# The rest of the modulation as reductions by output column on VectorE, and the low part of every third weight piece on GpSimd

## The reference, cut to what matters

```
mod   = silu(c)     @ w_mod[l] + b_mod[l]
mod_c = silu(c_ctx) @ w_mod[l] + b_mod[l]
shift, scale, gate = split(mod, 3)
x = rms_norm(h, pre_norm_g[l]) * (1 + scale) + shift
...
h = h + gate * rms_norm(y, post_norm_g[l])
```

## Time and profile before

| | |
|---|---|
| three runs | median 3389.24 us (3387.71 to 3394.56) |
| the profiled execution | 3387.43 us, span 3385.6 us, mean granted clock 0.929 |
| TensorE busy | 3040.6 us (90%) |
| VectorE busy | 1966.1 us (58%) |
| ScalarE busy | 1109.5 us (33%) |
| GpSimd busy | 784.2 us (23%) |

### The profile page before, as it was taken

The page is one execution under the profiler, slowest core; times in us unless marked ns, Lnnn a source line. Parts: engine busy times, 40 slices in busy tenths (PEclk is TensorE's granted clock), DMA queues, the critical chain, the costliest instruction groups (busy, mean ns, idle before and its releaser), DMA issues.

```text
span 3385.6 us, 40936 instructions
## 1 busy us (share of the span) xinstructions
PE 3040.6 (90%) x15813; PEld 2449.2 (72%) x15813; DVE 1966.1 (58%) x2774; ACT 1109.5 (33%) x1774; POOL 784.2 (23%) x641
## 2 busy tenths in 40 slices
PE   6789778989978997998998996987999999999998
PEld 1167567777766886767786785764588999999887
DVE  5477876666665544444525455877554666666444
ACT  2132322322312323332423243222343444444443
POOL 0068448577462000000000000655200000000000
PEclk9989889989988999999999997988589899999999
DMA  8844224244333453323333253432033455555655
GB/s 310 279 141 155 75 97 146 97 143 146 110 121 109 171 170 113 116 78 107 108 101 114 78 184 103 142 98 77 14 120 129 141 185 181 186 182 182 197 194 168
DMA packets 148802, 471.19 MB, mean 139 GB/s; under 512 B 16752, under 2 KB 17776, under 8 KB 147440
## 3 DMA queue, kind: packets, MB, share of 16 engines
q1 hardware_dynamic: 137664, 431.03, 38.9%
q10 hardware_dynamic: 8384, 28.63, 2.2%
q0 software_dynamic: 2560, 8.91, 0.8%
HBM read 455.40 MB, written 13.11 MB: 138 GB/s over the span
## 4 chain that ended last, share of the span: by engine, by line
PE 56%; issue 18%; DVE 11%; POOL 7%; DMA 4%; ACT 3%; ACTq 0%; DVEq 0%; POOLq 0%; SPq 0%
PE bank L906 15%; PE bank L907 15%; PE bank L908 15%; POOL first_block_work L2306 3%; DMA common<-w_mod 2%; POOL common L2304 2%; DVE split_weights L1227 2%; PE bank L923 2%; ACT split_weights L1884 1%; DVE first_block_work L1325 1%; PE bank L1020 1%; PE bank L943 1%; PE bank L1098 1%; PE bank L1001 1%; DMA first_block_work<-w_mod_rows 1%
## 5 line engine op out<-in xcount | busy, mean ns | idle before, releaser
L1227 DVE TENSOR_TENSOR split_weights<-common,split_weights 128x1024 fp32r<-128x1024 f32 x628 | 831.5, 1332 | 789.1 <-ACT split_weights L1884 778.5
L1884 ACT ACTIVATE split_weights<-common 128x1024 fp32r<-128x1024 f32 x628 | 656.6, 1053 | 1155.5 <-PE bank L908 1098.0
L906 PE MATMUL bank<-split_weights,features 128*128 128x512 f32 x1920 | 820.6, 427 | 16.3 <-DVE features L1370 10.1
L907 PE MATMUL bank<-split_weights,features 128*128 128x512 f32 x1920 | 770.0, 401 | 0.0
L908 PE MATMUL bank<-split_weights,features 128*128 128x512 f32 x1920 | 769.3, 401 | 0.0
L2276 POOL TENSOR_TENSOR common<-common 128x1 f32<-128x1 f32 (+4 forms) x54 | 39.5, 739 | 1888.6 <-DVE common L1830 752.2
L906 PEld LDWEIGHTS bank<-split_weights,features 128*128 128x128 f32 x1920 | 375.0, 195 | 124.8 <-issue 37.0
L908 PEld LDWEIGHTS bank<-split_weights,features 128*128 128x128 f32 x1920 | 373.3, 194 | 82.7
L907 PEld LDWEIGHTS bank<-split_weights,features 128*128 128x128 f32 x1920 | 374.9, 195 | 79.6 <-issue 11.8
L906 PE MATMUL bank<-ffn_input_split,split_weights 128*128 128x256 f32 (+1 forms) x1376 | 393.1, 286 | 2.8 <-DVE ffn_input_split L1650 1.6
L907 PE MATMUL bank<-ffn_input_split,split_weights 128*128 128x256 f32 (+1 forms) x1376 | 391.6, 285 | 0.0
(11 more groups left out here) (282 smaller groups left out, 3677.2 us busy)
## 6 DMA issues: line engine op xcount, KB each, us to landing
common<-w_in SPq DMA_DIRECT2D x252, 512.0 KB, 3.4
common<-w_up SPq DMA_DIRECT2D x172, 512.0 KB, 4.2
first_block_work<-w_mod_rows SPq DMA_DIRECT2D x256, 256.0 KB, 3.6
common<-w_out SPq DMA_DIRECT2D x96, 512.0 KB, 3.3
common<-w_down SPq DMA_DIRECT2D x84, 512.0 KB, 3.3
common<-w_mod SPq DMA_DIRECT2D x64, 512.0 KB, 4.9
trig<-common ACTq DMA_DIRECT2D x32, 272.0 KB, 5.1
second_block_work<-trig POOLq DMA_DIRECT2D x32, 272.0 KB, 3.4
```

Source lines behind the costliest of these rows:

```text
L906: e.matmul(out_ap, xs[0], ws[0], start=first, stop=False)
L907: e.matmul(out_ap, xs[1], ws[0], start=False, stop=False)
L1227: e.tensor_tensor(lo, raw, hi.bitcast(F32), ALU.subtract).then_inc(*low_done.tick(("lo", m)))
L1884: e.activation(split_slots[:, 0, i, 0:words], raw_slots[:, m % RAW, 0:words], ACT.Copy).then_inc(*high_done.tick(("high", m)))
```

## The change

`w_mod` is given transposed. A piece now has 128 outputs on the partitions and a quarter (512) of the inputs along the row, and silu(c) of both streams, the same quarter of it, stands in every partition (`silu_rows`, 128 x 1024). One `tensor_tensor_reduce` of VectorE (L1336) multiplies piece and row and adds the sum over the row to one column of `mod_all`; the first of an output's four starts from the bias. There is one for each stream that is needed. TensorE's column sums, VectorE's additions after them and GpSimd's rows are gone. The 256 loads of 256 KB remain.

The rows of silu are made anew for each quarter, 7 times (layer 1 begins with the quarter that layer 0 ended on): ScalarE loads 512 KB once VectorE has read the last piece of the round before (`silu_load`), then for each stream ScalarE takes a tanh and VectorE two steps (`silu_row`, L1324, L1327).

Shift, scale and gate of layer 1 are now all complete with the last piece; before, scale was complete after two thirds. In the list of steps the last piece lies 60 steps ahead of the end of layer 0's projections.

The low part of each piece m with m % 3 = 2 goes to GpSimd (L2308) up to piece 351: 48 pieces in each layer, always in the same raw and the same split slot.

```diff
@@ -123,6 +125,11 @@
 START = (None, 0)
 
 
+def on_gpsimd(m):
+
+    return m % 3 == 2 and m < MOD_PIECES + DEPTH * (INC + 4) * KT // KP
+
+
 class Events:
 
 
@@ -338,25 +345,33 @@
         return self.steps
 
     def modulation(self):
-        todo = [(0, c, k) for c in range(MOD_FIRST, MODC) for k in range(KT)]
-        todo += [(l, c, k) for l in range(1, DEPTH) for c in range(MODC) for k in range(KT)]
+        rounds = [(0, q, range(2 * KT, 3 * KT)) for q in range(4)]
+        rounds += [(l, q, range(3 * KT)) for l in range(1, DEPTH) for q in reversed(range(4))]
+        todo = [(l, j, q) for l, q, blocks in rounds for j in blocks]
         for i in range(MODRING - 1):
             self.do("mod_load", i, *todo[i])
-        for i, (l, c, k) in enumerate(todo):
-            with_ctx = l < DEPTH - 1 or c < MOD_FIRST
-            self.do("mod_row", i, l, c, k, with_ctx)
-            if i + MODRING - 1 < len(todo):
-                self.do("mod_load", i + MODRING - 1, *todo[i + MODRING - 1])
-            yield
-            if k == KT - 1:
-                self.do("mod_column", i, l, c, with_ctx)
-                if c == MOD_FIRST - 1:
-                    self.do("mod_scale", l)
+        i, row, held = 0, -1, None
+        for l, q, blocks in rounds:
+            if q != held:
+                row, held = row + 1, q
+                self.do("silu_load", row, q, i)
+                yield
+                for s in range(2):
+                    self.do("silu_row", row, s)
+                    yield
+            for j in blocks:
+                first = q == (3 if l else 0)
+                self.do("mod_piece", i, l, j, first, row, l < DEPTH - 1 or j < 2 * KT)
+                if i + MODRING - 1 < len(todo):
+                    self.do("mod_load", i + MODRING - 1, *todo[i + MODRING - 1])
+                i += 1
+                yield
+            if q == (0 if l else 3):
+                if l:
+                    self.do("mod_scale", l, i - 1)
                     self.reached.add(("scale", l))
-                if c == MODC - 1:
-                    self.do("mod_gate", l)
-                    self.reached.add(("gate", l))
-                yield
+                self.do("mod_gate", l, i - 1)
+                self.reached.add(("gate", l))
 
     def normed(self, l):
         self.turn += 1
@@ -761,15 +776,15 @@
     rows_buf = [W.one(CH) for _ in range(2)]
     scratch = W.one(CH)
     silu_c = W.two(KT, 2)
-    mod_ring = W.two(MODRING, CH)
-    mod_acc = [W.one(CH) for _ in range(2)]
+    mod_ring = W.two(MODRING, QUARTER)
+    silu_rows = W.two(2, QUARTER)
     subln = W.one(HD)
     qk_g = W.two(2, HD)
     H = Room(h_t_words, KT * T2)
     probs_a = [H.one(CH) for _ in range(2)]
     probs_b = H.one(CH)
     probs_t = [H.one(CH) for _ in range(2)]
-    mod_tmp = H.one(CH)
+    mod_junk = H.one(QUARTER)
     lam_words = H.one(4 * SUB)
     turn_a, turn_b = H.one(CH), H.one(CH)
     ssq, rstd = small.one(NT * 4), small.one(NT)
@@ -933,16 +947,6 @@
             names = [("mod_turned", c)] + ([("scratch", 0)] if c == MOD_FIRST - 1 else [])
             done.then_inc(*modulation_turned.tick(*names))
 
-        def mod_column(i, l, c, with_ctx):
...
-
         def normed_turn(l, f, x):
             tb = banks[4 + f % 4]
             for s, n in seen.new(tb.claim("normed", l, f)):
@@ -1220,6 +1224,8 @@
             e.tensor_scalar(silu_c, silu_c, 0.5, None, ALU.mult).then_inc(*modulation_scaled.tick(("silu",)))
 
         def low(m):
+            if on_gpsimd(m):
+                return
             i, words = (m - MOD_PIECES) % HALVES, plan[m].shape[-1]
             raw, hi, lo = raw_slots[:, m % RAW, 0:words], split_slots[:, 0, i, 0:words], split_slots[:, 1, i, 0:words]
             for s, n in seen.new(at("raw", m), at("high", m), at("used", m - HALVES) if m >= MOD_PIECES + HALVES else START):
@@ -1311,42 +1317,43 @@
                             bc(vecs[:, b0:b0 + 4], 2, (P, 4, 2)), ALU.add).then_inc(
                 *modulation_added.tick(("mod_added", 0, c), ("free", "mod_turn", c)))
 
-        def mod_row(i, l, c, k, with_ctx):
...
-
-        def mod_column(i, l, c, with_ctx):
-            b0 = VEC["b_mod"][0] + l * 3 * KT + 4 * c
-            for s, n in seen.new(at("mod_summed", i // KT)):
-                e.wait_ge(s, n)
-            e.tensor_tensor(mod_all[l][:, 4 * c:4 * c + 4, :], banks[6][:, 0:8].rearrange("p (j s) -> p j s", s=2),
-                            bc(vecs[:, b0:b0 + 4], 2, (P, 4, 2)), ALU.add).then_inc(
-                *modulation_added.tick(("mod_added", l, c), ("free", "mod_column", l, c)))
-
-        def mod_scale(l):
+        def silu_row(row, stream):
+            words = silu_rows[:, stream, :]
+            for s, n in seen.new(at("silu_row_tanh", row, stream)):
+                e.wait_ge(s, n)
+            e.scalar_tensor_tensor(out=words, in0=mod_junk, scalar=1.0, in1=words, op0=ALU.add, op1=ALU.mult).then_inc(
+                *modulation_scaled.tick())
+            e.wait_ge(*modulation_scaled.last())
+            e.tensor_scalar(words, words, 0.5, None, ALU.mult).then_inc(*modulation_scaled.tick(("silu_row", row, stream)))
+
+        def mod_piece(i, l, j, first, row, with_ctx):
+            for s, n in seen.new(at("mod_in", i), at("silu_row", row, 1)):
+                e.wait_ge(s, n)
+            for stream in range(2 if with_ctx else 1):
+                total = mod_all[l][:, j, stream:stream + 1]
+                for s, n in seen.new(modulation_added.last()):
+                    e.wait_ge(s, n)
+                e.tensor_tensor_reduce(out=mod_junk, in0=mod_ring[:, i % MODRING, :], in1=silu_rows[:, stream, :], scale=1.0,
+                                       scalar=col("b_mod", l * 3 * KT + j) if first else total, op0=ALU.mult, op1=ALU.add,
+                                       accum_out=total).then_inc(
+                    *modulation_added.tick(*[("mod_read", i)] * (stream == with_ctx)))
+
+        def mod_scale(l, i):
             g0 = VEC["pre_g"][0] + l * KT
-            for s, n in seen.new(at("mod_added", l, MOD_FIRST - 1)):
+            for s, n in seen.new(at("mod_added", l, MOD_FIRST - 1) if i is None else at("mod_read", i)):
                 e.wait_ge(s, n)
             e.tensor_scalar(scaled_g[l], mod_all[l][:, KT:2 * KT, :], 1.0, None, ALU.add).then_inc(*modulation_scaled.tick())
             e.wait_ge(*modulation_scaled.last())
             e.tensor_tensor(scaled_g[l], scaled_g[l], bc(vecs[:, g0:g0 + KT], 2, (P, KT, 2)), ALU.mult).then_inc(
                 *modulation_scaled.tick(("scales_ready", l)))
 
-        def mod_gate(l):
-            gate = mod_all[l][:, 2 * KT:, :]
-            for s, n in seen.new(at("mod_added", l, MODC - 1)):
-                e.wait_ge(s, n)
-            e.tensor_tensor(gate, gate, bc(vec("post_g")[:, l * KT:(l + 1) * KT], 2, (P, KT, 2)), ALU.mult).then_inc(
+        def mod_gate(l, i):
+            streams = 2 if l < DEPTH - 1 else 1
+            gate = mod_all[l][:, 2 * KT:, 0:streams]
+            for s, n in seen.new(at("mod_read", i)):
+                e.wait_ge(s, n)
+            e.tensor_tensor(gate, gate, bc(vec("post_g")[:, l * KT:(l + 1) * KT], 2, (P, KT, streams)),
+                            ALU.mult).then_inc(
                 *modulation_scaled.tick(("gates_ready", l)))
 
         def normed_turn(l, f, x):
@@ -1920,6 +1928,17 @@
         def tables_end():
             for s, n in seen.new(at("coefficients", "ci"), at("table_stored", SJ - 2), at("table_stored", SJ - 1)):
                 e.wait_ge(s, n)
+
+        def silu_load(row, q, i):
+            for s, n in seen.new(at("mod_read", i - 1) if i else START):
+                e.wait_ge(s, n)
+            e.dma_start(silu_rows, A["c_rows"][q]).then_inc(*rows_loaded.tick(("c_row", row)))
+
+        def silu_row(row, stream):
+            for s, n in seen.new(at("c_row", row), at("silu_row", row, 0) if stream else START):
+                e.wait_ge(s, n)
+            e.activation(mod_junk, silu_rows[:, stream, :], ACT.Tanh, scale=0.5).then_inc(
+                *tables_made.tick(("silu_row_tanh", row, stream)))
 
         def normed_turn(l, f, x):
             if f % 2 == 0:
@@ -2279,6 +2298,15 @@
             for s, n in seen.new(at("vectors"), at("consts"), at("consts_1")):
                 e.wait_ge(s, n)
 
+        def low(m):
+            if not on_gpsimd(m):
+                return
+            i, words = (m - MOD_PIECES) % HALVES, plan[m].shape[-1]
+            raw, hi, lo = raw_slots[:, m % RAW, 0:words], split_slots[:, 0, i, 0:words], split_slots[:, 1, i, 0:words]
+            for s, n in seen.new(at("raw", m), at("high", m), at("used", m - HALVES) if m >= MOD_PIECES + HALVES else START):
+                e.wait_ge(s, n)
+            e.tensor_tensor(lo, raw, hi.bitcast(F32), ALU.subtract).then_inc(*low_done_too.tick(("lo", m)))
+
         def scale_rows(l, t):
             for s, n in seen.new(at("row_mean", l, t)):
                 e.wait_ge(s, n)
```

(12 more changed lines are left out.)

51 lines of the change are left out of this document (11 added, 40 removed).

## The result

The change takes 3261.61 us (median of four, 3257.5 to 3266.5) beside 3388.47 of the kernel before on the same chip: ratio 0.9627, 95% interval 0.9604 to 0.9650. That is 127 us less, where 65 were forecast. The direction was right. The time lies outside the range (3273 to 3372) and is nearest to rival (c), 3266.

What follows compares the result with a forecast made beforehand. The prediction took GpSimd falling behind TensorE in layer 0, with TensorE's waits and lowered clock, as the bound. Its terms -40 - 30 - 20 - 10 + 15 + 12 + 8 = -65 gave 3322 us, range 3273 to 3372.

Steps and rivals of the forecast that it cites:

- rival (c): More waiting and clock time comes back in layer 0 and only 10 us is lost: -121, 3266 us; chance 0.12.
- What bounds the kernel: Layer 0: GpSimd falls behind TensorE, which stands still 132 of 1172 us and partly runs at the lower clock.
- Part 2: GpSimd loses 180 pairs of row instructions, so head turns no longer stand behind rows in its queue: -10 us.
- part 1: TensorE's column sums go: matmuls -40, idle time before them -30, lower clock around them -20 us.
- Part 3: VectorE: rows and some low parts out, 448 reductions in, busy sum 770 us as now; delay beside attention +15 us.
- The clock: Dips of TensorE's clock around the column sums, some six of 16 places: -20 us, bounds 0 and -50.
- Parts 3 to 5: Costs added: VectorE's reduction trains +15, silu rows made 7 times +12, low parts on GpSimd +8 us.
- part 5: 48 low parts on GpSimd in each of layers 0 and 1, delaying its queue: +8 us, between -10 and +40.
- rival (a): VectorE's reduction in layer 0 runs at half rate, 1.69 us a pair: +63, 3450 us; chance 0.09.
- The rule against the change: GpSimd's low parts could block VectorE for whole instructions, 139 us in layer 0 instead of 9: forecast some 15 us higher.
- (b): VectorE's reduction trains and the silu rows eat most of the gain: 3355 to 3378 us; chance 0.17.
- (d): Nothing moves: gains and losses cancel within 0.2%; chance 0.05.

Runs made afterwards that it cites:

- no_sums: The kernel before with TensorE's 16 column sums left out and GpSimd's rows kept: 3305.7 us, ratio 0.9764.
- both out: The kernel before without TensorE's column sums and without GpSimd's context rows: 3234.6 us, ratio 0.9550.
- heads_on_vector: The change with all low parts left on VectorE and the head turns' subtraction and addition moved from GpSimd to VectorE: 3235.9 us, ratio 0.9544.
- columns_alone: The change with all low parts left on VectorE, none on GpSimd: 3253.8 us, ratio 0.9599; timed again, 3255.2 us, 0.9595.

## Why the prediction was right in direction and wrong in size

*What bounds the kernel: right.* All but 5 us of the gain lies in layer 0, in the three things named there: the sums, GpSimd's lag, the clock.

*Part 2, GpSimd's rows, -10: **the step that failed***. Taken in the forecast's order, part 1 is no_sums: 80 us measured beside 90 forecast (40 + 30 + 20). Taking the rows out after that gave 71 us, where part 2 had 10. It counted only that the head turns no longer stand behind rows in GpSimd's queue. The runs put some 19 of the 71 on the queue, and some 52 on VectorE's instructions, which took longer beside the rows' own two-input ones (1169 ns for 753, 1691 for 1225). Part 3 had the lengthened times in its rows and used them for VectorE's busy sum alone, where they are worth little, since VectorE was not full. Where TensorE waits at the end of a chain through VectorE, each shorter instruction is time: the waits on VectorE and ScalarE were 87 us with the rows and 52 with memsets in their place. No run lengthened VectorE's instructions in these chains alone, so how the 52 spread over them stays open.

*Part 1: 80 of 90, but not by its three terms.* In layer 0 the matmuls' work was 28 us, not 40, since the 40.3 were partly lower clock; the prediction saw that for one place (3.55 against 1.92 us) and took it from the clock's term. The idle time fell by 14, not 30: with the sums out TensorE waited 54 us before the head turns, 39 before, and 19 before the first matmul of a triple, 13 before. The lost clock fell by 33, not 20. That the sum came near is in part luck.

*The clock, -20 in all: too small by half.* It was 44 us with both out, and 35 to 41 in the change. The term was scaled from the dip around a sum, "some six of the 16 places", which no row shows. Taking the rows out alone gave 42 back, taking the sums out after them 2: the lower clock went with the waits, and the term was small for the same reason as part 2. Rival (c)'s measure, 0.09 of 890 us and 0.02 of 282, 86 us, counts the lower clock while TensorE stood still, too; what was lost beyond the idle time was 69.

*Parts 3 to 5, +35: near, 27 to 29.* The change stands at 3261.6 or 3263.3, the kernel without either half at 3234.6. Columns on VectorE with the silu rows cost 19 to 21 (15 + 12 predicted; of it some 3 for the silu rows, not clear of noise), the low parts 8 (8 predicted). That last agreement is luck: part 5 had the queue of GpSimd in both layers for it, and most of what was measured lies in layer 0, where the low parts hold VectorE's reductions. The reduction's pair was 0.94 us, 0.84 without GpSimd beside it: the taken 0.90 was the right end, and rival (a) fell with it. The Trainium skill, Vector Engine (DVE) Microarchitecture Reference, Points that are easy to get wrong, has `S2S2D2_STT`, the form of scalar_tensor_tensor, at half throughput with two such sources (SBUF, not bf16). The rows of that instruction, without accumulator, took 752 ns with GpSimd silent, only 22% more than half of a low part of twice the elements (1225 ns); that disagrees. The reduction, 755 ns, is a custom instruction in the trace; no run has the page's form with its accumulator.

*The rule against the change: right where the prediction said never.* The Trainium skill, SBUF - State Buffer, Who interferes with whom, has one engine hold the other for a whole instruction, and the reduction of 2.81 us beside a low part of 2.40 agrees with it. The lengthening of the reductions was 46.5 us in all, between the 9 taken and the 139 by the rule, as not every low part meets one at its start. TensorE paid 8 for it, of the 15 that the rule would have added.

*Rivals.* (a), (b) and (d) fell. (c) gave 3266 by gains of 131 with 10 lost; in fact some 151 were gained and 27 lost, so its time came near with both sides too small, which is luck in part.

## What to carry to other kernels

Work that leaves a second engine on shared memory is worth more than the waits on that engine show: read how long the first engine's instructions are with the second silent, and price the difference where the first is awaited. Take the clock's term from the whole stretch, as half of the time that TensorE is busy at the lower level (69 us of 1199 here), and not from the dip that is easiest to see; (1 - granted clock) times the length (96 us here) counts again what is already in the idle time. And before a stand-in is believed, compare its pace in the queue with that of the work it replaces: 0.37 us a row too much turned a 19 us effect into 64.

## What the runs showed of the hardware

- An accumulating reduction of 128x512 on VectorE took 750 to 755 ns with GpSimd silent (heads_on_vector, columns_alone), no more than the row without accumulator (752 with both out), and its accumulator's read 82 ns, under half of ScalarE's 193.
- The cost of GpSimd's queue turned steep with its pace: stand-ins 3.08, 3.29 and 3.61 us apart gave 4, 19 and 64 us over no rows (7, 22 and 60 by the ratios).
- GpSimd's memset of 128x512 (528 ns) left VectorE's two-input instructions at 753 and 1225 ns; its two-input ones brought them to 1169 and 1691.
- Eight narrow matmuls at each of 16 places, waiting for no data, cost TensorE 28 us of work and no clock; its lower clock went with the waits (GpSimd's rows out: 69 to 27 us lost; the sums out after them: 27 to 25).
